# Another order of the experts in a streamed mixture-of-experts stage, and three experts in place of four ahead of the sorted ones

## The reference, cut to what matters

```python
g_prob = jax.nn.softmax((t @ rg_w + rg_b).astype(jnp.float32), axis=-1)
g_p, g_idx = lax.top_k(g_prob, 1)
e_p, e_idx = lax.top_k(jax.nn.softmax(e_logits, axis=-1), MOE_TOPK)
expert = (g_idx * MOE_EPG + e_idx).reshape(-1).astype(jnp.int32)
def expert_block(args):
    xb, e = args
    hg, hu = jnp.split(xb @ w_gu[e], 2, axis=-1)
    return (jax.nn.silu(hg) * hu) @ w_down[e]
out = jax.ops.segment_sum(y, tok_buf, num_segments=n_tok + 1)[:n_tok]
```

## Time and profile before

| what | value |
|---|---|
| median of 3 runs | 3465.34 us (3461.54 to 3467.52) |
| the profiled execution | 3461.82 us, its span 3460.1 us |
| PE busy | 3004.1 us, 87% |
| DVE, ACT, POOL busy | 39%, 26%, 8% |
| HBM read | 611 MB, 184 GB/s over the span |
| first load of the ring, layer 0 and layer 1 | 1882.01 and 2913.58 us |
| first product of an expert | 1922.6 and 2955.6 us |
| copy of the last block | 2412.8 and 3422.1 us |

### The profile page before, as it was taken

How to read it: one execution, slowest core, us unless ns; L and a number is a source line. 1 busy time by engine, 2 the same in 40 slices (tenths; PEclk the granted TensorE clock), 3 DMA queues, 4 the chain that set the end, 5 groups by cost and what they waited for, 6 DMA issues and landing times. The chain is left out here.

```text
span 3460.1 us, 79809 instructions
## 1 busy us (share of the span) xinstructions
PE 3004.1 (87%) x34143; PEld 2295.5 (66%) x34143; DVE 1339.7 (39%) x2527; ACT 895.0 (26%) x1656; POOL 284.8 (8%) x361
## 2 busy tenths in 40 slices
PE   6998889999898899999977798865799898899876
PEld 4755567878773678787755677744367866677753
DVE  3254434332555343322173322211578544322222
ACT  2244422221335221212262110000443333111001
POOL 1013310000303000000000000000210430000000
PEclk8999999999999899999998899987799999999987
DMA  7423223324325233232213989998212214999996
GB/s 200 89 86 147 98 45 102 95 75 109 85 61 203 81 99 97 77 105 89 74 51 132 426 331 381 410 426 354 94 55 81 57 34 164 427 402 421 424 426 275
DMA packets 375788, 639.16 MB, mean 185 GB/s; under 512 B 90436, under 2 KB 327665, under 8 KB 339449
## 3 DMA queue, kind: packets, MB, share of 16 engines
q1 hardware_dynamic: 350025, 601.98, 47.9%
q10 hardware_dynamic: 21264, 23.88, 2.0%
q0 software_dynamic: 4256, 9.68, 0.8%
HBM read 611.06 MB, written 24.38 MB: 184 GB/s over the span
## 5 line engine op out<-in xcount | busy, mean ns | idle before, releaser
L1943 PE MATMUL moe_ps<-moe_ring,moe_scratch 128*32 128x128 f32 x12928 | 429.2, 290 | 137.0 <-DMA moe_ring<-in_moe_w_gu 82.7
L1943 PEld LDWEIGHTS moe_ps<-moe_ring,moe_scratch 128*32 128x32 f32 x12928 | 391.3, 117 | 181.8 <-issue 110.3
L212 PE MATMUL ffn_in_ps<-ffn_xhi,ffn_in_whi 128*128 128x512 f32 x704 | 280.3, 398 | 8.3 <-DVE ffn_xlo L408 8.3
L2134 DVE TENSOR_TENSOR moe_scratch<-moe_scratch,moe_ps 128x64 f32<-128x64 f32 x204 | 54.7, 268 | 600.6 <-ACT moe_scratch L2003 600.6
L213 PE MATMUL ffn_in_ps<-ffn_xlo,ffn_in_whi 128*128 128x512 f32 x704 | 279.8, 397 | 0.0
L214 PE MATMUL ffn_in_ps<-ffn_xhi,ffn_in_wlo 128*128 128x512 f32 x704 | 279.6, 397 | 0.0
L1927 PE MATMUL moe_ps<-xT,moe_hot 128*32 128x256 f32 x3296 | 228.8, 402 | 17.9 <-issue 17.9
L1953 PE MATMUL moe_ps<-moe_ring,moe_scratch 128*32 128x256 f32 x3232 | 212.4, 382 | 9.9 <-issue 9.8
L1927 PEld LDWEIGHTS moe_ps<-xT,moe_hot 128*32 128x32 f32 x3296 | 137.4, 117 | 71.6 <-issue 36.5
L2003 ACT ACTIVATE moe_scratch<-moe_ps 128x64 f32<-128x64 f32 x204 | 44.9, 224 | 517.6 <-PE moe_ps L1943 458.1
L1953 PEld LDWEIGHTS moe_ps<-moe_ring,moe_scratch 128*32 128x32 f32 x3232 | 130.0, 111 | 68.2 <-issue 18.5
(11 more groups left out here) (724 smaller groups left out, 5651.5 us busy)
## 6 DMA issues: line engine op xcount, KB each, us to landing
moe_ring<-in_moe_w_gu SPq DMA_DIRECT2D x128, 2048.0 KB, 23.7
moe_ring<-in_moe_w_down SPq DMA_DIRECT2D x64, 2048.0 KB, 23.3
ffn_came<-in_ffn_w_in SPq DMA_DIRECT2D x88, 512.0 KB, 5.0
na_modw<-in_ada_w SPq DMA_DIRECT2D x6, 4096.0 KB, 13.6
rga_modw<-in_ada_w SPq DMA_DIRECT2D x16, 1024.0 KB, 6.0
expert_rows<-moe_y ACTq DMA_DIRECT2D x408, 32.0 KB, 6.5
da_in_w<-in_attn_w_qkv SPq DMA_DIRECT2D x12, 1024.0 KB, 5.2
ro_w<-in_rw_w_rkv SPq DMA_DIRECT2D x24, 512.0 KB, 3.7
```

What stands on the lines that cost most here:

```text
L212: nc.tensor.matmul(ps[0:width, slot * tiles + o], high, xhi[:, k], start=(k == 0), stop=False)
L1943: last = nc.tensor.matmul(psGU[j * BLK:(j + 1) * BLK, a], xbT[:, k], cols[:, j], start=(k == 0), stop=(k == KD - 1))
L2134: V.tensor_tensor(h[:, a].rearrange("p (m i) -> p i m", m=2), gated[:, a].rearrange("p (i m) -> p i m", m=2), psGU[:, a, HD:P].rearrange(" ...
```

## The change

FIXED goes from 4 to 3. Unit 9, the first part of the expert at place 3, is then no longer known ahead: SP loads it, like the rest, when the plan is there, and the wait for `normed` falls away. The other 29 experts get their places by a fold: rank r below 15 goes to 2r, rank r from 15 on to 57 - 2r, so that the largest stands next to the smallest, the second largest next to the second smallest, and so on. VectorE needs four chained operations for that in place of two.

```diff
             turn, turnT, later, over = (L[:].rearrange("p c n -> p (c n)")[:, 32 * i:32 * i + 32] for i in range(4))
+            upper = where[:, 0]
             psRank, psBegin, psPlan = ps[:, 3, 128:160], ps[:, 3, 160:192], ps[0:1, 3, 192:256]
-            FIXED = UNITS // PARTS + 1
+            FIXED = UNITS // PARTS
...
                 for u in range(UNITS - 1):
                     load(u, u // PARTS)
-                sp.wait_ge(normed, KD)
-                load(UNITS - 1, FIXED - 1)
                 sp.wait_ge(plan_ready, 1)
-                for u in range(UNITS, PARTS * EXPERTS):
+                for u in range(UNITS - 1, PARTS * EXPERTS):
                     q, part = (u - UNITS) // PARTS, (u - UNITS) % PARTS
                     if u % PARTS == 0:
                         e = expert_at(sp, u // PARTS)
-                    if part != 1:
+                    if part != 1 and u >= UNITS:
                         end = end_of(sp, q)
                         sp.wait_ge(down_done if part == 2 else gu_done[1], end)
-                    load(u, e if u // PARTS >= FIXED else u // PARTS)
+                    load(u, e)
...
                 dve.wait_ge(rank_summed, 1)
-                half = (EXPERTS - FIXED) // 2
-                link(V.tensor_scalar(over[:], psRank, float(half), float(2 * half - 1), ALU.is_ge, ALU.mult))
-                link(V.scalar_tensor_tensor(out=turn[:, some], in0=psRank[:, some], scalar=2.0, in1=over[:, some], op0=ALU.mult, op1=ALU.subtract))
+                behind = (EXPERTS - FIXED + 1) // 2
+                fold = float(4 * behind - 3) if (EXPERTS - FIXED) % 2 else float(4 * behind - 1)
+                link(V.tensor_scalar(over[:], psRank, float(behind), None, ALU.is_ge))
+                link(V.tensor_scalar(upper[:], psRank, -4.0, fold, ALU.mult, ALU.add))
+                link(V.tensor_tensor(over[:], over[:], upper[:], ALU.mult))
+                link(V.scalar_tensor_tensor(out=turn[:, some], in0=psRank[:, some], scalar=2.0, in1=over[:, some], op0=ALU.mult, op1=ALU.add))
```

## The result

The changed kernel takes 3480.66 us (median of 5 runs, 3478.06 to 3481.14), the one before 3462.29 us in the same comparison. The ratio is 1.0049, with a 95% interval of 1.0037 to 1.0060: slower by some 17 us (18.4 between the two medians). The forecast was 12.5 us slower, 3477.5 us.

The account below looks back on a forecast made before the run. The prediction took the weights' stream, which stands still where the ring is full, to set the end. Its terms, 5.3 + 6.3 + 0.9 = +12.5 us, gave 3477.5 us by the median, range 3467 to 3488.

Parts of the forecast that it names:

- The stream sets the end, and a standstill is what it loses: Expert stages: the weights' stream sets the end and loses time where the ring is full, 17.4 us in layer 0.
- SP's long wait begins 12 us earlier: Sign in the trace after: SP's wait for layer 0's seven-block expert begins some 12 us earlier.
- The fold moves nothing: Order of ranked experts: the partner's block count stays the same, so the fold by itself costs 0 us.
- Unit 9 costs nothing: Unit 9's load waits for the plan, to about 1919, but the queue has work until 1926: cost 0.
- VectorE +0.45 a layer: Two more chained operations between rank_summed and placed: +0.45 us a layer, +0.9 in all.
- Three units less t1: Heavy experts one place earlier: three units' transfer (15.3) less one single-block expert's PE time, +5.3 and +6.3 us.
- Over many places the phase of the gaps averages out: First passes on TensorE: gaps average out, so mean t1 is taken, 10.0 us in layer 0, 9.0 in layer 1.
- One of the prediction's own signs of being wrong: The prediction is wrong if the pairs of layer 0 fall below 32 us.
- The rival "faster": Heavies at odd places meet other code gaps; layer 0's pairs reach layer 1's pace, saving up to 18 us; chance 0.06.
- Only one layer pays: Rival: the stream, not the ring, ends layer 1, which gives about +1; total +5 to +7 us; chance 0.16.
- The rule of the Trainium skill: Crossing into new 16 KiB code blocks is mostly hidden: t1 7.3 us in both layers, +17 us; rival's chance 0.08.
- The sum: Whole kernel: +12.5 us on the profiled 3461.8 gives 3474.3; by the median, forecast 3477.5 us.

Follow-up runs that it names:

- every-third order: Kernel before, but ranked experts placed so only every third place has a heavy one, the first two places later: ratio 0.9941, 3440.51 us.
- the same two kernels: Kernels before and changed, each with tiny TensorE products moving both layers' code to the good position: 3451.81 us (0.9969) and 3469.90 us (1.0022).

## Why the prediction was right or wrong, point by point

The forecast of 12.5 us lies near the 17 measured, but in part by luck. It was made of +5.3 and +6.3 in two layers that moved by -0.4 and +18.7, and a mechanism that it held to average out moved each of them by as much as the place did or more.

- *The stream sets the end, and a standstill is what it loses.* Right. Where the windows lose bytes the layer gets longer, and the every-third order, which loses half as much at the seven-block expert, is the fastest.
- *SP's long wait begins 12 us earlier.* Right: 1953.22, where it was 1964.79, 11.6 us.
- *The fold moves nothing.* Right: 0.9991.
- *Unit 9 costs nothing.* Right: 0.9999, and 426 GB/s over the stretch in question. In the changed kernel it went out at 1921.14 in place of about 1919, and the stream moved 429 GB/s from 1902 to 1931.
- *VectorE +0.45 a layer.* Agrees: in layer 1 the first expert product followed the first load after 42.0 us and now does after 42.4.
- *Three units less t1.* It agrees as far as the stages tell. With the code's position taken out they give 6.2 and 5.6 us a layer; the forecast was 5.3 and 6.3, each with 0.45 on top. The medians of the same two kernels give 18 for the whole, with room down to 12. The standstill at the seven-block expert grew as it should. The forecast read 17.4 us lost from its window of 23 us, which cuts off both ends. Over 1970 to 2030 the stream moved 295 GB/s before and 252 in the changed kernel, so it lost (426 - 295) / 426 x 60 = 18.5 us and now loses 24.5, 6.0 more. In layer 1 the forecast also left out the window from 3060 to 3070, with 355 GB/s, and so put the standstill before at 3.3 us instead of 4.9; that only speaks more for its reading that the ring bounds there.
- *"Over many places the phase of the gaps averages out."* Wrong, and it is the step that failed. The position moves down by 14 or 15 products in two places, so over the four pairs that bind it moves by some 45 of 192 and does not average. A shift by one place took the four pairs of layer 1 from 124.7 to 141.3 us and those of layer 0 from 138.9 to 125.9. In the lengths of the stages that is +13.1 and -6.6. The sum of the two is +6.5, which would by itself explain why the stages lost 18 and not 12; the medians with moved code neither show nor exclude that sum. One of the prediction's own signs of being wrong came true as well: three of the four pairs of layer 0 are now below 32 us, such as 2113.43 - 2083.28 = 30.2.
- *The rival "faster".* Its mechanism was there, and in layer 0 it did what it said: the pairs came down to the pace of layer 1. Its price was too high: the four pairs gave 13.0 us in place of 18, and the length of the layer 6.6; why not all of the 13.0 arrive there was not measured. What spoke against the rival, that layer 1 can lose by the same exchange, was the larger part. The price of layer 1 should have been worked out from the same rows: 35.6 less 31.0 there, four times.
- *Only one layer pays.* It was so in the profile, but it was the other layer. Layer 1, which the rival held for slack, paid 18.7, and layer 0 moved by -0.4.
- *The rule of the Trainium skill* ("Runtime: NRT & Kernel Launch", "Instruction fetch mechanics"), that crossing into a new block of code is mostly hidden, does not hold here, where weights fill the DMA engines: moving such crossings within the passes of one layer cost 14 us in the run in which no expert moved.
- *The sum.* 3474.3 and the 3.5 us between that execution and the median give 3477.8 and not 3477.5, which changes nothing.

## What to carry to other kernels

Where a stream through a ring sets the time, an order of the work is worth what it saves in standstills. A heavy item one place earlier costs about the stream's time for one place less the compute time of one light item. Spreading the heavy ones behind enough light ones saved 20 us here. Code that is written out once per item is itself a stream, and part of its waits is for the data in the same DMA engines. When items with repeats change places with items without, work out the positions of the waits for code per place, and not their mean. Before an order is judged by a difference of half a percent, move the code by half a piece and look again.

## What the runs showed of the hardware that I had not expected

- The waits in TensorE's code stand at fixed positions. Moving the code of one layer by 114 instructions gives 1.0041, by 256 it gives 0.9995; 256 instructions fit as the size of a piece, and an instruction packet has 16.4 KB.
- With full DMA engines, a first pass in layer 1 took 7.2 us where it met no such wait (place 15 before) and 12.5 where it met 1.20 and 2.58 us of them (place 7 in the changed kernel). Behind a wait of 2.6 to 2.8 us the next products run slower for a while: the gather takes 3.20 and 3.33 us where it takes 1.94. The granted clock is 0.61 in the 4 us from 3069 of the changed kernel and 1.00 in the 3 us behind them; in the run with the code of before moved it is 0.57 from 3083 to 3087. So a wait for code costs a second time, by the clock.
- With the stream at a quarter of its bytes, the first passes of places 1 to 15 are still 8.0 us long, where a repeat takes 6.95: a part of the wait is not queueing behind the weights.
